# Expert passes in 1024-wide weight blocks, with the V pass turned round and sample rows gathered

## What is computed

```python
q = (xb @ w_q).reshape(PEER_BLOCK, PEER_HEADS, 2, D_KEY // 2)
s = jnp.einsum('thpc,pnc->thpn', q, sub_keys).astype(jnp.float32)
sv, si = lax.top_k(s, PEER_TOPK)
cand = (sv[:, :, 0, :, None] + sv[:, :, 1, None, :]).reshape(
    PEER_BLOCK, PEER_HEADS, PEER_TOPK * PEER_TOPK)
best, flat = lax.top_k(cand, PEER_TOPK)
...
idx = i1 * N_KEYS + i2
gate = jax.nn.softmax(best, axis=-1)
act = jax.nn.gelu(jnp.einsum('thkd,td->thk', u_tab[idx], xb).astype(jnp.float32),
                  approximate=False)
coef = (gate * act).astype(xb.dtype)
return jnp.einsum('thk,thkd->td', coef, v_tab[idx])
```

## Time and profile before

| | us |
|---|---|
| median of the runs | 1597.77 |
| the runs | 1597.32, 1597.77, 1600.88 |
| profiled execution, from its first to its last instruction | 1599.1 |
| in it: first query product | 494.4 |
| query pass | 494 to 568 |
| U pass A | 568 to 772 |
| U pass B | 772 to 1127 |
| V pass | 1129 to 1584 |
| tail | 1584 to 1599 |

### The profile page before, as it was taken

How to read it: one execution, slowest core, us unless ns; L and a number is a source line. 1 busy time by engine, 2 the same in 40 slices (tenths; PEclk the granted TensorE clock), 3 DMA queues, 4 the chain that set the end, 5 groups by cost and what they waited for, 6 DMA issues and landing times. The chain is left out here.

```text
span 1599.1 us, 33294 instructions
## 1 busy us (share of the span) xinstructions
PE 1477.0 (92%) x10641; PEld 1364.3 (85%) x10641; DVE 1053.5 (66%) x2356; ACT 629.8 (39%) x1401; POOL 381.5 (24%) x411
## 2 busy tenths in 40 slices
PE   6999757988796998898999999999999999999997
PEld 5987525876346998898999999999999999999997
DVE  4566896434433389994799999999544444544544
ACT  4423052320104554455544444444444444444443
POOL 1200140010101068987544444444000000000000
PEclk9999778999798999998999999999999999999998
DMA  6430200000403343343333333333444444444444
GB/s 219 139 108 25 114 15 1 1 27 2 188 25 118 113 124 119 119 138 110 104 121 118 118 118 118 118 119 120 142 144 150 152 144 153 149 145 154 147 147 142
DMA packets 87828, 181.02 MB, mean 113 GB/s; under 512 B 10144, under 2 KB 10656, under 8 KB 86752
## 3 DMA queue, kind: packets, MB, share of 16 engines
q1 hardware_dynamic: 87776, 180.32, 34.6%
HBM read 174.05 MB, written 6.22 MB: 113 GB/s over the span
## 5 line engine op out<-in xcount | busy, mean ns | idle before, releaser
L1628 PE MATMUL ph<-xh,hi 128*128 128x320 f32 x1152 | 370.7, 322 | 26.6 <-POOL lo L1532 19.9
L1532 POOL TENSOR_TENSOR lo<-raw,hi 128x256 fp32r<-128x256 f32 x352 | 318.3, 911 | 310.8 <-ACT hi L1548 295.9
L1629 PE MATMUL ph<-xl,hi 128*128 128x320 f32 x1152 | 360.5, 313 | 0.0
L1630 PE MATMUL ph<-xh,lo 128*128 128x320 f32 x1152 | 360.1, 313 | 0.0
L1879 PE MATMUL acc<-xh,hi 128*128 128x320 f32 x1024 | 317.2, 310 | 3.2 <-DVE lo L1865 3.2
L1548 ACT ACTIVATE hi<-raw 128x256 fp32r<-128x256 f32 x576 | 229.9, 416 | 221.5 <-PE ph L1630 211.6
L1880 PE MATMUL acc<-xl,hi 128*128 128x320 f32 x1024 | 317.1, 310 | 0.0
L1881 PE MATMUL acc<-xh,lo 128*128 128x320 f32 x1024 | 317.1, 310 | 0.0
L1628 PEld LDWEIGHTS ph<-xh,hi 128*128 128x128 f32 x1152 | 220.7, 192 | 34.4 <-POOL lo L1532 24.8
L1629 PEld LDWEIGHTS ph<-xl,hi 128*128 128x128 f32 x1152 | 220.8, 192 | 0.0
L1630 PEld LDWEIGHTS ph<-xh,lo 128*128 128x128 f32 x1152 | 220.4, 191 | 0.0
(11 more groups left out here) (352 smaller groups left out, 1829.8 us busy)
## 6 DMA issues: line engine op xcount, KB each, us to landing
raw<-in_uT SPq DMA_DIRECT2D x256, 256.0 KB, 2.7
raw<-in_v SPq DMA_DIRECT2D x256, 256.0 KB, 2.8
wraw<-in_w_in SPq DMA_DIRECT2D x30, 512.0 KB, 3.5
raw<-in_w_q SPq DMA_DIRECT2D x32, 256.0 KB, 2.7
wo<-in_w_out SPq DMA_DIRECT2D x4, 1024.0 KB, 10.8
sth<-in_state_h SPq DMA_DIRECT2D x1, 2048.0 KB, 8.0
out_hgrn_s<-stn SPq DMA_DIRECT2D x1, 2048.0 KB, 7.0
zm<-in_x_rows SPq DMA_DIRECT2D x3, 512.0 KB, 5.0
```

The source lines that it names most:

```text
L1532: pool.tensor_tensor(wide(lo[u % 4]), raw[u // 2][:, u % 2], wide(hi[u % 4]), ALU.subtract).then_inc(lo_pool, 1)
L1628: pe.matmul(o, hi[s][:, k], xh[:, c], start=begin, stop=False)
L1629: pe.matmul(o, hi[s][:, k], xl[:, c], start=False, stop=False)
L1630: ins = pe.matmul(o, lo[s][:, k], xh[:, c], start=False, stop=end)
```

## The change

- A weight block is loaded whole (512 KB, 1024 columns a partition) into one of four `raw` buffers, split by one ScalarE copy (`weight_high`) and one VectorE subtraction (`weight_low`) into one of two slots. A slot is free when TensorE has done the block two before. TensorE waits for `hi` first, runs 16 products, then waits for `lo` and runs 8.
- GpSimd makes no `lo` any more. In the query pass and pass A, VectorE makes them between the pieces of the search (`low()`); the first eight of each score group are searched in the query pass already.
- Pass A covers 64 blocks (NA), pass B 64 with gates for four tokens each: 256, the prompt's alone. `hid` holds 256 tokens.
- Sample tokens: their GELUs (64 columns a block, all 128 blocks) go to a scratch tensor in memory, eight blocks at a time, issued by ScalarE. VectorE forms row numbers from the chosen keys. In the V pass GpSimd issues indirect transfers: 64 of 128 single activations (`gather_act`) and 64 of 128 rows of `v` (`gather_v`, four buffers; four of them ahead of the activations). VectorE adds each row tile, times its coefficient, to `acc_s`: four in each eight blocks from the third step of eight on, eight in each of the last two steps. Two matmuls with `both` fold the 128 partitions to 64 tokens.
- V pass turned round: coefficients are the stationary operand (128 tokens), rows of `v` move, 512 columns at a time; 12 matmuls a block into four banks, tokens by features. The tail's copies and transposes are gone.
- 24 semaphores of an earlier stage are cleared and freed between two of its blocks, ahead of the output projection.

```diff
-        NQ, NA = 16, 48
...
+        NQ, NA, ST = 16, 64, 16
+        EXP_STEP, EXP_AT, PICK_AT = 3, 7, 12
+        TP = SEQ
+        NB = NBLK - NA
...
+        hid = big_mem.sb("hid", [P, NBLK, TP])
...
+
+        def weight_high(act, r, landed, slot, freed):
+            act.wait_ge(t_in[r], landed)
+            if freed is not None:
+                act.wait_ge(t_mm, freed)
+            act.activation(wide(hi[slot]), wide(raw[r]), ACT.Copy).then_inc(t_hi, 1)
+
+        def weight_low(dve, r, slot, highs):
+            dve.wait_ge(t_hi, highs)
+            dve.tensor_tensor(wide(lo[slot]), wide(raw[r]), wide(hi[slot]), ALU.subtract).then_inc(t_lo, 1)
...
+                    for r in range(4):
+                        sp.wait_ge(t_lo, 4 * i + (NQ - 3 + r))
+                        src = inp["uT"][bass.ds(4 * i + r, 1)]
+                        sp.dma_start(wide(raw[r]), src.rearrange("b p k n -> p (b k n)")).then_inc(t_in[r], 16)
...
-                def low(u, n):
-                    pool.wait_ge(t_hi, n)
-                    pool.tensor_tensor(wide(lo[u % 4]), raw[u // 2][:, u % 2], wide(hi[u % 4]),
-                                       ALU.subtract).then_inc(lo_pool, 1)
...
+                pool.memset(hflat[:, DIRTY:LATE], 1.0).then_inc(ones_set, 1)
+                pool.dma_start(idx_v[64:128], idx_u[0:64, 0, 64:128]).then_inc(idx_moved, 16)
...
+                    act.activation(hs[:, u // 8, u % 8], ph[:, q, TP:NT], ACT.Gelu).then_inc(hs_done, 1)
...
+                    act.dma_start(hs_dram[:, bass.ds(b0, 8)], hs[:, half]).then_inc(hs_out[half], 16)
...
+                            weight_high(act, u % 4, 16 * (NQ // 4) + 64 * s + (16 * (u // 4) + 16), u % 2,
+                                        ST * s + (NQ + u - 1))
...
+                def item(m, slot, q, highs):
+                    o = ph[:, q, 0:NT]
+                    pe.wait_ge(t_hi, highs)
+                    for c in range(KD):
+                        pe.matmul(o, hi[slot][:, c], xh[:, c], start=c == 0, stop=False)
+                        pe.matmul(o, hi[slot][:, c], xl[:, c], start=False, stop=False)
+                    pe.wait_ge(t_lo, highs)
+                    for c in range(KD):
+                        ins = pe.matmul(o, lo[slot][:, c], xh[:, c], start=False, stop=c == KD - 1)
                     ins.then_inc(t_mm, 1)
...
+                        if not (first and u < 2):
+                            pe.wait_ge(g_used, ST * s + (u - 1 - NA))
+                        pe.wait_ge(oh_ready, ST * s + (u + 1 - NA))
+                        for t in range(4):
+                            ins = pe.matmul(pg[:, u % 2, t], oh2[u % 2][:, t], oh1[u % 2][:, t], start=True, stop=True)
+                        ins.then_inc(g_mm, 1)
+                        pe.wait_ge(h_done, ST * s + (u - 1))
+                        item(None, u % 2, u % 2, ST * s + (NQ + u + 1))
...
+                for n in range(NQ + 2):
+                    low()
+                    if n >= 5:
+                        link(first_half(n - 5))
+                for m in range(NQ - 3, NQ):
+                    link(first_half(m))
+                    if m % 2:
+                        low()
...
+                for i, (c0, w) in enumerate(PT):
+                    for g in range(NQ):
+                        ins = dve.max(top[0:w, i, g, 8:16], sc[0:w, i, g])
+                        if g == NQ // 2 - 1:
+                            low()
+                    link(ins)
+                    low()
...
+                        link(dve.tensor_tensor(each, rankf[0:w, a].unsqueeze(3).to_broadcast(four),
+                                               iota[0:w, 0:TOPK].unsqueeze(1).unsqueeze(1).to_broadcast(four), ALU.is_equal))
+                        low()
+                        link(dve.tensor_tensor(each, each, keys(a).to_broadcast(four), ALU.mult))
+                        low()
+                        link(dve.tensor_reduce(picked[0:w, i, a].rearrange("p (h k) -> p h k", h=PH), each, AX, ALU.add))
...
+                    t0 = 4 * ST * s + (4 * u - 4 * NA)
+                    for t in range(4):
+                        dve.tensor_scalar(oh1[u % 2][:, t], iota[:], RT[:, 0, bass.ds(t0 + t, 1)],
+                                          RT[:, 2, bass.ds(t0 + t, 1)], ALU.is_equal, ALU.mult)
+                    dve.tensor_tensor(oh2[u % 2][:], iota[:].unsqueeze(1).to_broadcast([P, 4, NK]),
+                                      RT[:, 1, bass.ds(t0, 4)].unsqueeze(2).to_broadcast([P, 4, NK]),
+                                      ALU.is_equal).then_inc(oh_ready, 1)
...
+                def step_b(s, first):
+                    for u in range(ST):
+                        weight_low(dve, u % 4, u % 2, ST * s + (NQ + u + 1))
+                        one_hots(s, u, not (first and u < 2))
+                        if not (first and u < 1):
+                            times_gates(4 * ST * s + (4 * u - 4 - 4 * NA), (u - 1) % 2, ST * s + (u - NA),
+                                        None if first and u < 3 else ST * s + (u - 2 - NA))
+                        if not (first and u < 2):
+                            times_hidden(ST * s + (u - 2), u % 2, ST * s + (u - 1), ST * s + (u - NA))
+
+                dve.wait_ge(ones_set, 3)
+                dve.wait_ge(h_done, NA)
...
-                            o, s = acc[:, 4 * (u % 2) + k, 0:NT], u // 2
-                            pe.matmul(o, hi[u][:, k], ch[s], start=begin, stop=False)
-                            pe.matmul(o, hi[u][:, k], cl[s], start=False, stop=False)
-                            ins = pe.matmul(o, lo[u][:, k], ch[s], start=False, stop=end)
-                        ins.then_inc(v_mm, 1)
...
+                    pool.indirect_dma_start(vg[r][:], None, v_rows,
+                                            bass.IndirectOffsetOnAxis(ap=idx_v[:, j:j + 1], axis=0)).then_inc(vg_in[r], 16)
+
...
+                for j in range(4):
+                    gather_v(j, j, None)
+                for half in range(2):
+                    pool.wait_ge(hs_out[half], 16 * (NBLK // ST))
+                for j in range(64):
+                    gather_act(j)
+                for j in range(4, 64):
+                    gather_v(j, j % 4, j - 3)
...
+                                act.wait_ge(t_mm, 8 * s + (V0 + u - 2))
+                            act.activation(ch[u // 2 % 2], hid[:, bass.ds(8 * s + u, 2), :].rearrange("p b t -> p (b t)"),
+                                           ACT.Copy).then_inc(c_hi, 1)
+                        weight_high(act, u % 4, 32 * s + (4 * V0 + 16 * (u // 4) + 16), u % 2,
+                                    8 * s + (V0 + u - 1))
...
+                    dve.scalar_tensor_tensor(out=acc_s[:], in0=vg[r][:], scalar=coef[:, bass.ds(j, 1)], in1=acc_s[:],
+                                             op0=ALU.mult, op1=ALU.add).then_inc(s_added, 1)
...
+                def step(s, rows):
+                    for u in range(8):
+                        if u % 2 == 0:
+                            pair(s, u)
+                        weight_low(dve, u % 4, u % 2, 8 * s + (V0 + u + 1))
+                        if rows == 4 and u % 2:
+                            add_row(4 * s + (u // 2 - 8), u // 2, 16 * s - 16, 4 * s + (u // 2 - 8))
+                        if rows == 8:
+                            j = 8 * (s - 14) + 48 + u
+                            add_row(j, j % 4, 16 * (j // 4 + 1), j)
...
+                def products(a, b, begin, end):
+                    for i in range(2):
+                        for h in range(2):
+                            ins = pe.matmul(acc[:, i, h], a[:, P * i:P * i + P], b[:, 512 * h:512 * h + 512],
...
+                    a_hi, a_lo = (t[c][:, TP * sl:TP * sl + TP] for t in (ch, cl))
+                    w_hi_, w_lo_ = wide(hi[sl]), wide(lo[sl])
+                    if sl == 0:
+                        pe.wait_ge(c_hi, 4 * s + (u // 2 + 1))
+                    pe.wait_ge(t_hi, 8 * s + (V0 + u + 1))
+                    products(a_hi, w_hi_, begin, False)
+                    if sl == 0:
+                        pe.wait_ge(c_lo, 4 * s + (u // 2 + 1))
+                    products(a_lo, w_hi_, False, False)
+                    pe.wait_ge(t_lo, 8 * s + (V0 + u + 1))
+                    products(a_hi, w_lo_, False, end).then_inc(t_mm, 1)
...
+                pe.wait_ge(s_added, 64)
+                for h in range(2):
+                    ins = pe.matmul(psm[0:64, h], both[:], acc_s[:, 512 * h:512 * h + 512], start=True, stop=True)
```

More of the change, by code:

```diff
@@ L1621, in _ @@
+                samples_out(1, NBLK - 8, NBLK)
             @block.tensor
             def _(pe):
[L1623 to L1631 removed]
@@ L1652, in step_a @@
-                def step_a(i, first):
-                    for u in range(8):
-                        if u % 4 == 0 and not first:
-                            pe.wait_ge(h_done, 2 * i + (u // 4 - 1))
-                        pe.wait_ge(lo_pool, 8 * i + (u + 1))
```

(32 more changed lines are left out.)

656 lines of the change are left out of this document (313 added, 343 removed).

## The result

| | before, beside it | after |
|---|---|---|
| median, us | 1599.33 | 1493.95 (1485.8 to 1499.95) |
| ratio | | 0.934, 95% interval 0.930 to 0.938 |
| profiled execution, us | | 1490.2, span 1488.0 |

The forecast was 1485 in a range of 1453 to 1540. The page's totals (they answer) show TensorE with 128 us less work; 91% of a shorter span is busy. This is the first line under the page's heading for engines.

The account below looks back on a forecast made before the run. TensorE was taken as the bound, nearly alone in the V pass. Profiled sum: first product 496, query pass to 569, pass A with its end to 818, B to 1100, V to 1478, tail to 1487; less 1.3, 1485 us, range 1453 to 1540.

Parts of the forecast that it names:

- First product: Start of the query pass: first product at 494.4 + 1.6 = 496 us of the profiled execution.
- Query pass and pass A: From first product to first gates: query pass 73 us, pass A 225 + 18, its end 6, reaching 818.
- search stall: Pass A: TensorE waits for lo behind VectorE's wide search operations, 18 us for all three token tiles, bounds 5 and 30.
- The end of pass A: Wait for the last h_done ahead of the first one-hots: 5 us and a lower clock for a moment, 6 us.
- Pass B and border: 64 blocks of pass B at TensorE's pace, 282 us, then 3.6 us from last product to first V product.
- rival of unchanged one-hots: Pass B: one-hots stay at 539 ns, 5.4 us a block, 64 x 1.0 more, 1549 us; chance 0.09.
- V pass: 1536 products of 512 columns at 0.231 us, 355 us in all, plus 19 of gather stall.
- The price of a gather: GpSimd in the V pass: 0.74 + 0.6 = 1.3 us each, 69 issued before row 4, so 19 us stall.
- the two rules of the Trainium skill that I cited: V pass gathers: two-input VectorE operations hold up only GpSimd's reads; about 2.0 us fixed per transfer, 67 us stall if serial.
- The rival without the stall: V pass: GpSimd issues a gather in about 1 us undisturbed, so no stall, 1466 us; chance 0.22.
- Queues at the end: Last 16 V pass blocks: 378 GB/s wanted, queues suffice but for the last 44 us, 2 us inside the prefetch.
- Tail: After the V pass: copies out of acc and 24 transposes go, 6 us less, from 15.0 to 9.

Follow-up runs that it names:

- e9: Changed kernel plus useless GpSimd subtractions in pass A, as many as the kernel before made there for lo; 1513.75 us, one execution.
- e3: Changed kernel with gate_s formed by a VectorE product of two inputs in place of a copy; median 1484.28 us, ratio 0.925.
- e4: Changed kernel with GpSimd's memset of 13568 columns moved behind three small transfers, the copy kept; 1481.46 us, one execution.
- e6: Changed kernel with the first one-hots made ahead of the wait for the last GELU of pass A; median 1485.95 us, ratio 0.927.
- e10: Changed kernel plus two useless GpSimd memsets of 128 x 1024 for each block of pass B; 1508.35 us, one execution.
- e7: Changed kernel plus two useless GpSimd subtractions of 128 x 256 for each block of pass B; 1533.53 us, one execution.
- e1: Changed kernel with the V pass gathers reordered, so that later activation gathers are spread among the row gathers; median 1468.41 us, ratio 0.916.

## Why the prediction was right, and where its terms cancelled

The sum came to 1487 and the span to 1488.0. The V pass gained as foretold, but that the total agrees to about 1 us is luck: part by part the sum was 3 and 3 us too high, then 3, 1 and 4 too low.

- **First product**: 496 forecast, 493.06 measured, and 491.7 to 503.0 in other executions: within what this part varies by.
- **Query pass and pass A**: 322 forecast (818 - 496), 318.8 measured. The search stall is mis-sized: not 18 us but three gaps of 1.4 to 1.5, 4.3 in all. I summed with 2.76 us for a wide operation; those rows carried GpSimd's old work, which the change removes, and without it they take 2.28 to 2.29. e9 puts as many operations back and gets 4.0 to 5.3 us a tile back. For the one-hots I had looked for a row that GpSimd did not touch, for the search not; that is the step that failed. Against it stood a wait that the sum lacked, 6.93 us of a copy under a memset, 8.1 with its clock (e3, e4). So 14 us too much stood against 8 too little. The end of pass A was right: 6 forecast, 4.84 plus a low clock measured, and e6 shows its cause.
- **Pass B and border**: 286 forecast (282 + 3.6), 288.2 measured; behind the wait at the end of pass A the clock is low for a moment (granted 0.51 from 811 to 818 us), and e6, without that wait, has 285.5. (355 / 80 less 3.52 is 0.92, not the 0.89 that I summed with; the 4.41 us a block that came bears out the 0.89.) No gap inside, VectorE's cover is thin but holds, and from the first of four one-hots to the comparison it is 1.03 us, thus 0.26 each, as I took. The rival of unchanged one-hots falls here. That longer ones cost time is shown, but not at its price of 64 us: e10, with one-hots listed at 583 ns, even above its 539, takes 9.2 us more in this pass, and e7 35 with `lo` stretched as well.
- **V pass**: 374 forecast, 374.9 measured. e1 splits it: 349.7 for 1536 products, 0.228 each (forecast 355, 0.231 each from the earlier trace rows), and a stall of 25.3 with its clock where I had 19. Here too two errors, of 5 and 6 us, nearly cancel. The gap came 73 us into the pass, once, by the path foretold. The price of a gather, 1.3 us, was nearly right for a wrong reason: I put it together as 0.74 for the work and 0.6 for waiting on VectorE. It is 0.94 and 0.30 between two, 1.25, with VectorE standing still, and 64 of them take (66.0 + 19.5) / 64 = 1.34 over all, so VectorE's part is about 0.1. Row 4 was added 3.4 us after its issue had ended (1191.74 to 1195.18), where I had 2.5. So the two rules of the Trainium skill that I cited fare thus. By the Trainium skill's "SBUF — State Buffer", section "Who interferes with whom", operations with two inputs leave the writing of descriptors alone; that is nearly so here, but not wholly: each of the 64 that took more than 0.95 us (up to 1.45) began while such an operation ran. The conclusion that no stall follows was mine and wrong, as a gather costs 1.25 us by itself. The 2.0 us of the Trainium skill's "DMA: Bandwidth & Descriptors", section "Anatomy of one DMA — SWDGE (gpsimd) path", are not paid one after another, as the 1.25 show. The rival without the stall was priced at 1466; e1, which takes the stall away, has 1468.4.
- **Queues at the end**: the last 75 us ran at share 0.93 and 324 GB/s, with no TensorE gap, as forecast (378 wanted only in the last 44).
- **Tail**: 9 forecast, 12.8 measured from the end of the last product. I took off all of the 1.70 and 4.49 us of the earlier trace rows. But in the kernel before, the first sum did not wait for the transposes of all tiles (VectorE there, in order of time):

```profile
1587.54 1.22 DVE L1934 TENSOR_TENSOR hid<-hid,acc 128x1024 f32<-128x1024 f32 x1 [1.74 <-PE acc L1923]
```

From that sum to the end it took 11.6 us, now 1488.0 - 1476.4 = 11.6 too. Only what stood ahead of the first sum could go. The wait for the load of `norm_f` adds 0.9 in this execution; others have none.

## What to carry over

A duration read from a trace holds for the work that ran beside it: when the change removes that work, look for a row of the same operation without it, for every term of the sum. A queue that issues in order is paid by what stands ahead of the first item somebody waits for, so put the items in the order of need; that alone gave 25 of the 41 us that were still to be had here. And where one engine has free time, ask of each instruction form what it blocks: a copy of 64 columns cost 8 us where a product of the same size cost 0.22. That is a matter of the form and not of the number of inputs alone, as the reciprocal of 0.20 under the same memset shows.

## What the hardware did that I had not expected

- A VectorE copy of 64 x 64 stood 8.09 us under a GpSimd memset that reads nothing, and one-hots (one input) went from 341 to 583 ns beside memsets, while `lo` (two inputs) kept 1225 ns. Beside GpSimd subtractions, `lo` took up to 1.77 us.
- With VectorE standing still, an indirect gather of 128 rows occupies GpSimd for 0.94 us and the next begins 0.30 later, whether a row has 4 bytes or 4 KB; the row that VectorE waited for was added 4.4 us after its issue (1190.80 to 1195.18).
- Behind a gap of 24 us the clock came back within the next stretch: 1.3 us of the V pass were lost to it, beside the gap itself.
